# Items of 96 rows in a mixture-of-experts block, and the overflow branch behind the final norm

## The chip, the cores and the metric

The kernel runs on one core of one Trainium2 chip. The metric is device time in microseconds (us) of that core, the median of three runs.

## What is computed

One trunk layer over 512 tokens of width 1024, in float32: an input norm, a combined projection, eight heads of forgetting attention and eight of stick-breaking attention, an output projection added to the input, then a mixture of experts added to that, and a last norm. The change touches the mixture and the last norm. Cut to these:

```python
logits = t @ w_router + b_router              # 512 tokens, 32 experts
top_v, top_i = lax.top_k(logits, 4)           # each token goes to 4 experts
top_w = softmax(top_v)
# per expert e, on the rows (tokens) that chose it, however many they are:
hh  = x @ w1[e] + b1[e]                       # 1024 -> 2048
glu = minimum(hh[:, :1024], 7.0)
lin = clip(hh[:, 1024:], -7.0, 7.0)
act = glu * sigmoid(1.702 * glu) * (lin + 1.0)
y   = (act @ w2[e] + b2[e]) * weight_of_row   # 1024 -> 1024, added to its tokens
out = rmsnorm(x2 + sum of y, norm_f_g)
```

An expert gets 64 rows on average (512 x 4 / 32).

## The kernel before

**Items.** The mixture runs as a list of items, one expert's weights and up to 128 of its rows each. `run_items(MAIN)` does items 0 to 31, item e being the first 128 rows of expert e. An expert with more than 128 rows leaves the rest to items 32 and up, `run_items(REST)`, which stand in a branch that is entered only if the fullest expert has more than 128 (`fullest` writes 0 or 1 into `novi`; every engine loads that value and branches).

**One item.** GpSimd gathers the rows from `tn_scratch` with an indirect DMA (L655, indices in `gtab`; a row that doesn't exist has an index past the last token and isn't moved). TensorE turns them (`turn_x`, L2139, eight transposes of 128 columns), ScalarE copies the result to `xT_hi` rounded (L1063, L1066), VectorE writes the remainder `xT_lo` (L1596). The weights arrive in float32 in `ring` (SyncE's queue) in pieces of 128x1024; ScalarE casts each to `stage_hi` (L783), VectorE subtracts to get `stage_lo` (L1203), and `multiply` (L2189) runs six matmuls of 512 columns with it: T_hi with hi, T_lo with hi, T_hi with lo, for two banks. An item has 16 pieces of w1 and 8 of w2. Between them stand the clips (L1632, L1636), the gate (L1085), `gated` (L1644, the product), `turn_a` (L2147, eight transposes), `a_evac` (L1079) and again L1596. `y_evac` (L1093) scales by the row's weight into `yout` and GpSimd adds the rows to `x_scratch` (called `x2_d`) in memory: a copy of the indices to `sidx` (L662) and an indirect DMA (L666), then a wait for its landing.

**The order.** Each engine has its instructions in program order; the order of pieces and of the small operations between them is written by hand (`body(r)`, with `if j == ...`). The w2 pieces of item t-1 follow the w1 pieces of item t.

**The end.** The last item isn't scattered. Its result is kept on chip as `y_hi` (`last_high`, ScalarE L1168) and `y_lo` (`last_low`, VectorE L1718), and for each of four tiles of 128 tokens TensorE adds the second biases (`second_biases`, L2272) and the rows of the last item picked by a one-hot matrix (`last_expert`, L2294) in PSUM. When GpSimd has seen item 30 land and has passed the branch, it sets `all_scattered` (L772), and SyncE loads the four tiles of `x2_d` (`total(t)`, L582). VectorE adds PSUM to each (`added`, L1756), ScalarE takes the sum of squares and the root (L1185, L1187), VectorE scales (`final`, L1762, L1763), SyncE stores (L585). The branch for REST stands, on every engine, ahead of this part; on TensorE between the second biases and `last_expert`:

```python
pe.wait_ge(over_known, 1)
n_over = pe.value_load(novi[0:1, 0:1], min_val=0, max_val=1)
with pe.If(n_over > 0):
    ...                       # items 32 and up
pe.wait_ge(onehot_r, TT)
pe.wait_ge(y_ready, E)
for t in range(TT): ...       # last_expert
```

Of the kernel before, what the change touches and what calls it, by code (L numbers as in the profile page):

```python
# [20 lines left out]
F32 = mybir.dt.float32  # L21
# [30 lines left out]
OVER = S * TOPK // P - 1  # L52
# [78 lines left out]
def build(nc, x, norm1_g, w_in, b_f, g_fox, g_sb, w_out, norm2_g, w_router, b_router, w1, b1, w2, b2,  # L131
# [6 lines left out]
    with ExitStack() as ctx:  # L138
# [32 lines left out]
        gtab = sb("gtab", [P, ITEMS], I32)  # L171
        wtab = sb("wtab", [P, ITEMS])
        seltab = sb("seltab", [P, ITEMS + OVER])
        eidtab = sb("eidtab", [1, 16], I32)
        novi = sb("novi", [1, 1], I32)
        gidx = sb("gidx", [P, 1], I32)
        sidx = sb("sidx", [P, 1], I32)
        wcol = sb("wcol", [P, 1])
        last_rows = sb("last_rows", [P, 1])
# [51 lines left out]
        onehot = over("onehot", [P, S], F32R, room_at + 7168)  # L231
# [7 lines left out]
        ohslot = over("ohslot", [P, 16, P], F32R, qk_at + 16 * S)  # L239
        over_slot = in_slot("over_slot", [P, 16, P], F32R, 8)  # L240
# [14 lines left out]
        y_hi = act_hi[:, 2 * D:3 * D]  # L255
        y_lo = act_lo[:, 2 * D:3 * D]
        g2b = slot(8)[:, 0:D]
        small = slot(8)[:, D:2 * D]
        gath = qk2[:, 0, :]
        glu = qk2[:, 1, :]  # L260
        lin = qk2[:, 2, :]
        sig = qk2[:, 3, :]
        yout = qk2[:, 4, :]
# [22 lines left out]
        counts = part(2007, 32)  # L286
        most = part(2039, 1)
# [161 lines left out]
        def _(sp):  # L449
# [100 lines left out]
            sp.dma_start(gfb, norm_f_g.rearrange("(a d) -> a d", a=1).partition_broadcast(P)).then_inc(gf_in, 16)  # L550
            sp.wait_ge(over_known, 1)
# [26 lines left out]

            sp.wait_ge(split_lo, MAIN.split(E - 1, W1P + W2P - 1))
            sp.wait_ge(all_scattered, 1)  # L580
            for t in range(TT):
                sp.dma_start(total(t), x2_d[t * P:(t + 1) * P, :]).then_inc(fin_in[t], 16)  # L582
            for t in range(TT):
                sp.wait_ge(fin_ready, t + 1)
                sp.dma_start(out_d[t * P:(t + 1) * P, :], total(t)).then_inc(out_done, 16)  # L585
# [5 lines left out]
        def _(pool):  # L591
# [156 lines left out]
            def last_scatter():  # L748

                pool.wait_ge(y_ready, E)  # L750
                nc.gpsimd.tensor_copy(sidx[:], gtab[:, E - 1:E]).then_inc(sidx_copied, 1)
# [20 lines left out]
            nc.gpsimd.memset(gidx[:], 0).then_inc(all_scattered, 1)  # L772
# [3 lines left out]
        def _(act):  # L776
# [282 lines left out]
            def x_evac(t):  # L1059

                early = isinstance(t, int) and t == 0
                act.wait_ge(*((x_half, 1) if early else (x_turned, t + 1)))
                nc.scalar.copy(xT_hi[:, 0:4, :], bank[6][:].rearrange("p (k t) -> p k t", k=4)).then_inc(xT_hi_r, 1)  # L1063
                if early:
                    act.wait_ge(x_turned, 1)
                nc.scalar.copy(xT_hi[:, 4:8, :], bank[7][:].rearrange("p (k t) -> p k t", k=4)).then_inc(xT_hi_r, 1)  # L1066

            def x_next(t, h, used_at):

                if h == 0:  # L1070
                    act.wait_ge(x_turned, t + 1)
                else:
                    act.wait_ge(used, used_at)
                nc.scalar.copy(xT_hi[:, 4 * h:4 * h + 4, :], bank[6 + h][:].rearrange("p (k t) -> p k t", k=4)).then_inc(xT_hi_r, 1)

            def a_evac(t, halves=(0, 1)):
                act.wait_ge(a_turned, t + 1)
                for h in halves:
                    nc.scalar.copy(aT_hi[:, 4 * h:4 * h + 4, :], bank[6 + h][:].rearrange("p (k t) -> p k t", k=4)).then_inc(aT_hi_r, 1)  # L1079
# [7 lines left out]
            def y_evac(t, used_at):  # L1087
# [4 lines left out]
                for h in range(2):  # L1092
                    ins = nc.scalar.activation(yout[:, h * BANK:(h + 1) * BANK], bank[4 + h][:], ACT.Copy,  # L1093
# [3 lines left out]
            def run_items(run):  # L1097
# [7 lines left out]
                for j in range(W1P):  # L1105
                    if j == STAGES:
                        x_evac(q0)
                        if b == MOE0:
                            act.wait_ge(wt_mm, 1)
                            nc.scalar.copy(wtab[:, 0:E], bank[1][:, 0:E]).then_inc(wt_copied, 1)  # L1110
# [38 lines left out]
                for j in range(W2P):  # L1149
# [13 lines left out]
            def last_high(used_at):  # L1163
# [3 lines left out]
                for h in range(2):  # L1167
                    nc.scalar.activation(y_hi[:, h * BANK:(h + 1) * BANK], bank[h][:], ACT.Copy, scale=wcol[:]).then_inc(last_hi, 1)  # L1168
# [4 lines left out]
            nc.scalar.copy(b2r[0:96, :], b2raw[0:96, :]).then_inc(b2_hi, 1)  # L1173
            act.wait_ge(over_known, 1)
            n_over = act.value_load(novi[0:1, 0:1], min_val=0, max_val=1)
            last_high(MAIN.base - OPROJ_PIECES + 24 * E)
            with act.If(n_over > 0):
                act.wait_ge(over_copied, 1)
                nc.scalar.copy(wtab[:, E:ITEMS], bank[5][:, P + WIDE:P + WIDE + OVER]).then_inc(over_copied, 1)
                run_items(REST)  # L1180

            nc.scalar.preload_act_table_set("sqrt_and_others")
            for t in range(TT):
                act.wait_ge(fin_added, t + 1)
                nc.scalar.activation(squares(t), total(t), ACT.Square, accum_out=ss3[:, t:t + 1]).then_inc(fin_sq, 1)  # L1185
                act.wait_ge(fin_sq, t + 1)
                nc.scalar.activation(rs3[:, t:t + 1], ss3[:, t:t + 1], ACT.Sqrt, scale=1.0 / D, bias=epsc).then_inc(fin_rs, 1)  # L1187
# [3 lines left out]
        def _(dve):  # L1191
# [297 lines left out]
            def slots(g):  # L1489
# [10 lines left out]
                nc.vector.tensor_tensor(ohslot[:, a], iotas[:].unsqueeze(1).to_broadcast([P, TOPK * n, P]),  # L1500
# [824 lines left out]
```

## Time and profile before

| | |
|---|---|
| median of three runs | 1477.76 us (1477.41 to 1479.73) |
| the profiled execution's own time | 1478.53 us |
| its span, first to last instruction | 1476.8 us |
| TensorE busy | 1448.6 us, 98% |
| VectorE busy | 1323.5 us, 90% |
| ScalarE busy | 1114.6 us, 75% |
| mean granted TensorE clock | 0.993 |

Engines in the rows are PE (TensorE), PEld (its weight loads), DVE (VectorE), ACT (ScalarE), POOL (GpSimd) and SP (SyncE). A share of busy time is a mean over the attention, the routing, the 32 items and the end. The span runs from the first instruction to the last; 1.7 us of the execution's time lie outside it.

### The profile page before, as it was taken

What the parts mean: (1) busy time and instruction counts of PE and PEld (TensorE: products, weight loads), DVE (VectorE), ACT (ScalarE), POOL (GpSimd) and SP (SyncE); (2) the same over time, 40 slices, a digit from 0 to 9 for tenths busy, and PEclk for the clock granted to TensorE, in tenths of its full rate; (3) what the DMA queues carried; (4) which work ended last, traced back from release to release, by engine and by line L of the source; (5) the groups of instructions that cost most, each with busy time, mean ns of one, the idle gap of its engine ahead of it and who ended that gap; (6) DMA issues with size and microseconds to landing.
All of it is one profiled execution on the core that took longest, in us unless ns stands there. A gap on an engine that the chain in (4) does not pass through costs nothing.

```text
span 1476.8 us, 22343 instructions
## 1 busy us (share of the span) xinstructions
PE 1448.6 (98%) x7069; PEld 1180.6 (80%) x7069; DVE 1323.5 (90%) x1520; ACT 1114.6 (75%) x1345; POOL 325.4 (22%) x179
## 2 busy tenths in 40 slices
PE   9999999999999999999999999999999999999996
PEld 7777787787888888888888888888888888888884
DVE  5778656569999999999999999999999999999997
ACT  5668545357888888888888888888888888878885
POOL 3000000141322222222222233233222222222210
PEclk9999999989999999999999999999999999999998
DMA  8021122369999999999999999999999999999963
GB/s 258 22 65 57 30 94 67 129 225 418 417 383 384 378 378 374 375 370 376 375 369 375 374 369 380 365 371 389 367 361 373 373 378 369 369 372 379 370 220 125
DMA packets 100074, 451.32 MB, mean 306 GB/s; under 512 B 13443, under 2 KB 25731, under 8 KB 67266
## 3 DMA queue, kind: packets, MB, share of 16 engines
q1 hardware_dynamic: 90706, 434.16, 76.8%
q0 software_dynamic: 9328, 16.64, 4.5%
q8 instruction: 23, 0.38, 0.1%
q14 instruction: 17, 0.14, 0.0%
HBM read 444.66 MB, written 22.54 MB: 316 GB/s over the span
## 4 chain that ended last, share of the span: by engine, by line
PE 85%; DVE 7%; ACT 3%; DMA 2%; issue 2%; POOL 0%; SPq 0%; POOLq 0%; ACTq 0%; DVEq 0%
PE zpair L2189 46%; PE bank L2189 23%; PE bank L1889 2%; PE bank L1777 2%; PE bank L2139 2%; PE bank L2147 2%; PE bank L1779 2%; PE bank L1778 2%; DVE stage_lo L1203 1%; DVE lbuf L1283 1%; PE zpair L2158 1%; DVE pt_lo L1292 1%; DMA tn_scratch<-qk 1%; ACT stage_hi L783 1%; DMA ring<-x_scratch 0%
## 5 line engine op out<-in xcount | busy, mean ns | idle before, releaser
L1203 DVE TENSOR_TENSOR stage_lo<-ring,stage_hi 128x1024 fp32r<-128x1024 f32 x796 | 945.9, 1222 | 37.9 <-ACT stage_hi L783 8.3
L783 ACT CAST stage_hi<-ring 128x1024 fp32r<-128x1024 f32 x796 | 828.2, 1054 | 169.8 <-PE zpair L2189 139.0
L2189 PE MATMUL zpair<-stage_hi,act_hi 128*128 128x512 f32 x1024 | 322.5, 396 | 0.0
L2189 PE MATMUL zpair<-stage_lo,act_hi 128*128 128x512 f32 x1024 | 316.2, 390 | 0.4 <-DVE stage_lo L1203 0.3
L2189 PE MATMUL zpair<-stage_hi,act_lo 128*128 128x512 f32 x1024 | 316.0, 390 | 0.0
L2189 PEld LDWEIGHTS zpair<-stage_lo,act_hi 128*128 128x128 f32 x1024 | 192.1, 188 | 41.8 <-DVE stage_lo L1203 1.3
L2189 PEld LDWEIGHTS zpair<-stage_hi,act_lo 128*128 128x128 f32 x1024 | 192.2, 188 | 40.9
L2189 PEld LDWEIGHTS zpair<-stage_hi,act_hi 128*128 128x128 f32 x1024 | 187.2, 188 | 43.4 <-issue 7.9
L662 POOL COPY sidx<-gtab 128x1 int32 (+1 forms) x31 | 122.4, 3947 | 378.2 <-ACT qk L1093 378.2
L2189 PE MATMUL bank<-stage_hi,act_hi 128*128 128x512 f32 x512 | 161.2, 396 | 0.0
L2189 PE MATMUL bank<-stage_hi,act_lo 128*128 128x512 f32 x512 | 158.6, 391 | 0.0
L2189 PE MATMUL bank<-stage_lo,act_hi 128*128 128x512 f32 x512 | 157.8, 389 | 0.0
L666 POOL DMA_INDIRECT x_scratch<-qk,sidx x31 | 129.6, 4179 | 25.0 <-POOL sidx L662 25.0
L2189 PEld LDWEIGHTS bank<-stage_lo,act_hi 128*128 128x128 f32 x512 | 96.1, 188 | 21.1 <-DVE stage_lo L1203 0.4
L2189 PEld LDWEIGHTS bank<-stage_hi,act_lo 128*128 128x128 f32 x512 | 96.4, 188 | 20.5
L2189 PEld LDWEIGHTS bank<-stage_hi,act_hi 128*128 128x128 f32 x512 | 94.0, 189 | 17.6
L651 POOL COPY gidx<-gtab 128x1 int32 (+1 forms) x31 | 6.1, 198 | 402.8 <-PE bank L2139 402.8
L1596 DVE TENSOR_TENSOR act_lo<-bank,act_hi 128x512 fp32r<-128x512 f32 x128 | 82.3, 683 | 4.9 <-ACT act_hi L1063 3.5
L1777 PE MATMUL bank<-act_hi,stage_hi 128*128 128x512 f32 x184 | 76.3, 415 | 1.9 <-DVE v_lo L1247 1.9
L1779 PE MATMUL bank<-act_hi,stage_lo 128*128 128x512 f32 x184 | 72.0, 391 | 0.0
L1778 PE MATMUL bank<-act_lo,stage_hi 128*128 128x512 f32 x184 | 71.9, 391 | 0.0
L675 POOL TENSOR_TENSOR qk<-ring 128x1024 f32<-128x1024 f32 x3 | 8.1, 2725 | 273.0 <-DVE ring L1352 273.0
(297 smaller groups left out, 1450.9 us busy)
## 6 DMA issues: line engine op xcount, KB each, us to landing
ring<-in_w SPq DMA_DIRECT2D x384, 1024.0 KB, 8.0
ring<-in_w_in SPq DMA_DIRECT2D x12, 1024.0 KB, 5.3
ring<-in_w_out SPq DMA_DIRECT2D x4, 1024.0 KB, 4.9
xs_all<-in_x SPq DMA_DIRECT2D x4, 512.0 KB, 6.5
ring<-in_x SPq DMA_DIRECT2D x4, 512.0 KB, 3.7
tn_scratch<-qk SPq DMA_DIRECT2D x4, 512.0 KB, 3.5
x_scratch<-ring SPq DMA_DIRECT2D x4, 512.0 KB, 3.8
ring<-x_scratch SPq DMA_DIRECT2D x4, 512.0 KB, 6.7
```

The costliest lines, as they stand in the source:

```text
L662: nc.gpsimd.tensor_copy(sidx[:], gtab[:, i:i + 1] if isinstance(i, int) else gtab[:, bass.ds(i, 1)]).then_inc(sidx_copied, 1)
L666: nc.gpsimd.indirect_dma_start(out=x2_d[:, :], out_offset=bass.IndirectOffsetOnAxis(ap=sidx[:, 0:1], axis=0), in_=yout, in_offset=None, bo ...
L783: nc.scalar.copy(dst, src).then_inc(split_hi, 1)
L1203: nc.vector.tensor_tensor(dst, src, hi_ap.bitcast(F32), ALU.subtract).then_inc(split_lo, 1)
L1596: nc.vector.tensor_tensor(dst_lo[:, 4 * h:4 * h + n, :], bank[6 + h][:, 0:n * P].rearrange("p (k t) -> p k t", k=n), dst_hi[:, 4 * h:4 * h ...
L1777: pe.matmul(dst, w_hi, m_hi, start=start, stop=False)
L1778: pe.matmul(dst, w_hi, m_lo, start=False, stop=False)
L1779: return pe.matmul(dst, w_lo, m_hi, start=False, stop=stop)
L1889: mm = pe.matmul(obank[m][:, kb * P:S], w[:, ph % 2, kb, :], x[:, m, 4 * kb:3 * kb + TT, :].rearrange("p i q -> p (i q)"), start=kb == 0 a ...
L2139: mm = pe.transpose(bank[6 + k // 4][:, k % 4 * P:(k % 4 + 1) * P], gath[:, k * P:(k + 1) * P], identF[:])
L2147: mm = pe.transpose(bank[6 + k // 4][:, k % 4 * P:(k % 4 + 1) * P], lin[:, k * P:(k + 1) * P], identF[:])
L2189: mm = pe.matmul(bank[b0 + h][:], w[:, k, :], m[:, j % STAGES, h * BANK:(h + 1) * BANK], start=start and w is T_hi and m is stage_hi, stop ...
```

## The change

The capacity of an item, `CAP`, becomes 96 rows instead of 128, and the branch is entered if the fullest expert has more than 96. Everything that has one partition per row of an item is cut to 96 partitions, and everything that has one column per row to 96 columns, with one exception: the stationary tiles of `multiply` keep 128 columns (`w[:, k, :]`), of which the last 32 hold what was there before, and the 32 output rows that follow from them are not read. The branch moves behind the final norm and store on every engine; if it is entered, totals, sums and stores are done a second time. The order of a few steps at the end changes. The core of the diff:

```diff
+CAP = 96
+OVER = S * TOPK // CAP
...
-        gath = qk2[:, 0, :]
+        gath = qk2[0:CAP, 0, :]
...          # likewise glu, lin, sig, yout, y_hi, y_lo, gtab, wtab, onehot; ohslot has CAP columns
-                    mm = pe.transpose(bank[6 + k // 4][:, k % 4 * P:(k % 4 + 1) * P], gath[:, k * P:(k + 1) * P], identF[:])
+                    mm = pe.transpose(bank[6 + k // 4][:, k % 4 * CAP:(k % 4 + 1) * CAP], gath[:, k * P:(k + 1) * P], identF[0:CAP, 0:CAP])
...          # turn_a the same; x_evac, x_next, a_evac, turned_lo on 4 x 96 columns
-                nc.vector.tensor_scalar(novi[:], most[0:1, :], float(P), None, ALU.is_gt).then_inc(over_known, 1)
+                nc.vector.tensor_scalar(novi[:], most[0:1, :], float(CAP), None, ALU.is_gt).then_inc(over_known, 1)
...          # SyncE: totals before its branch; it waits for the landing itself
+            sp.wait_ge(split_lo, MAIN.split(E - 1, W1P + W2P - 1))
+            sp.wait_ge(scattered, 16 * (E - 1))
+            totals(0)
             sp.wait_ge(over_known, 1)
             n_over = sp.value_load(novi[0:1, 0:1], min_val=0, max_val=1)
             with sp.If(n_over > 0):
+                sp.wait_ge(out_done, 16 * TT)
...
-            sp.wait_ge(split_lo, MAIN.split(E - 1, W1P + W2P - 1))
-            sp.wait_ge(all_scattered, 1)
...          # ScalarE, the last item's w2 pieces
                     if j == 2:
-                        act.wait_ge(used, ub + 24 * n - 8)
+                        y_evac(q0 + n - 2, ub + 24 * n - 8)
                         a_evac(q0 + n - 1, (1,))
-                    if j == 3:
-                        y_evac(q0 + n - 2, ub + 24 * n - 8)
...
+            nc.scalar.preload_act_table_set("sqrt_and_others")
+            last_high(MAIN.base - OPROJ_PIECES + 24 * E)
+            roots(0)
             act.wait_ge(over_known, 1)
             n_over = act.value_load(novi[0:1, 0:1], min_val=0, max_val=1)
-            last_high(MAIN.base - OPROJ_PIECES + 24 * E)
...          # VectorE, body of the last item
+                        if j == 22 and last:
+                            gated(t)
                 body(n - 1, last=True)
-                gated(q0 + n - 1)
...
+            last_low()
+            dve.wait_ge(gf_in, 16)
+            finals(0)
             dve.wait_ge(over_known, 1)
             n_over = dve.value_load(novi[0:1, 0:1], min_val=0, max_val=1)
-            last_low()
...          # TensorE
             for t in range(3):
                 second_biases(t)
+            pe.wait_ge(onehot_r, TT)
+            pe.wait_ge(last_hi, 2)
+            for t in range(2):
+                last_expert(t, y_hi)
+            pe.wait_ge(y_ready, E)
+            for t in range(2):
+                last_expert(t, y_lo)
+            for t in range(2, TT):
+                if t == TT - 1:
+                    second_biases(t)
+                last_expert(t, y_hi)
+                last_expert(t, y_lo)
             pe.wait_ge(over_known, 1)
             n_over = pe.value_load(novi[0:1, 0:1], min_val=0, max_val=1)
             with pe.If(n_over > 0):
```

`finals(n)`, `roots(n)` and `totals(n)` hold the loops of the final norm that stood outside functions before, with their semaphores counted up by n rounds.

## Rows read from the trace of the kernel before

**Rows 1.** The page, part 1: busy us, share, instructions of each engine.

```profile
PE 1448.6 (98%) x7069; PEld 1180.6 (80%) x7069; DVE 1323.5 (90%) x1520; ACT 1114.6 (75%) x1345; POOL 325.4 (22%) x179
```

**Rows 2.** Groups of TensorE, 500 to 1300 us: busy, mean ns | idle before.

```profile
L2189 PE MATMUL zpair<-stage_hi,act_hi 128*128 128x512 f32 x730 | 229.7, 396 | 0.0
...
L2139 PE MATMUL bank<-identF,qk 128*128 128x128 f32 x184 | 23.9, 273 | 0.0
L2147 PE MATMUL bank<-identF,qk 128*128 128x128 f32 x184 | 23.8, 272 | 0.0
```

**Rows 3.** Groups of VectorE, 500 to 1300 us.

```profile
L1203 DVE TENSOR_TENSOR stage_lo<-ring,stage_hi 128x1024 fp32r<-128x1024 f32 x547 | 649.7, 1221 | 23.0
L1596 DVE TENSOR_TENSOR act_lo<-bank,act_hi 128x512 fp32r<-128x512 f32 x92 | 59.0, 683 | 0.0
```

**Rows 4.** Timeline of TensorE at two places: start us, length us, out<-moving,stationary.

```profile
288.08 0.94 PE L1949 MATMUL bank<-ones,f_sum 128*128 128x1 f32 x8
288.89 0.49 PE L1777 MATMUL zpair<-act_hi,fox_hi 128*128 128x512 f32 x1
...
824.20 1.03 PE L2147 MATMUL bank<-identF,qk 128*128 128x128 f32 x8
824.99 0.71 PE L2189 MATMUL zpair<-stage_hi,act_hi 128*128 128x512 f32 x2
```

**Rows 5.** Timeline of GpSimd over one item.

```profile
801.62 1.06 POOL L655 DMA_INDIRECT qk<-tn_scratch,gidx  x1 [0.78 <-POOL gidx L651]
813.83 4.02 POOL L662 COPY sidx<-gtab 128x1 int32 x1 [11.16 <-ACT qk L1093]
818.66 4.23 POOL L666 DMA_INDIRECT x_scratch<-qk,sidx  x1 [0.81 <-POOL sidx L662]
836.77 1.06 POOL L655 DMA_INDIRECT qk<-tn_scratch,gidx  x1 [0.78 <-POOL gidx L651]
```

**Rows 6.** The page: GpSimd's DMA queue, and the stores (us to landing).

```profile
q0 software_dynamic: 9328, 16.64, 4.5%
...
out<-ring SPq DMA_DIRECT2D x4, 512.0 KB, 2.7
```

**Rows 7.** DMA of 555.5 to 567.5 us, the gather of item 8: packets, MB.

```profile
q0 software_dynamic: 144, 0.36, 7.6%
```

**Rows 8.** Timeline of VectorE at the end.

```profile
1435.54 5.76 DVE L1203 TENSOR_TENSOR stage_lo<-ring,stage_hi 128x1024 fp32r<-128x1024 f32 x5
1441.21 1.22 DVE L1644 SCALAR_TENSOR_TENSOR qk<-qk 128x1024 f32<-128x1024 f32 x1
...
1465.60 1.29 DVE L1756 TENSOR_TENSOR ring<-bank,ring 128x512 f32<-128x512 f32 x2 [0.57 <-DMA ring<-x_scratch]
...
1472.37 1.28 DVE L1763 SCALAR_TENSOR_TENSOR ring<-ring,cols,qk 128x1024 f32<-128x1024 f32 x1
```

**Rows 9.** Timelines of TensorE, ScalarE and GpSimd at the end, one after another.

```profile
1442.49 1.09 PE L2147 MATMUL bank<-identF,qk 128*128 128x128 f32 x8 [0.79 <-DVE qk L1644]
...
1459.73 1.11 PE L2294 MATMUL bank<-act_hi,onehot 128*128 128x512 f32 x2 [2.20 <-issue]
...
1445.05 0.59 ACT L1079 CAST act_hi<-bank 128x512 fp32r<-128x512 f32 x1
...
1446.48 1.28 ACT L1093 ACTIVATE qk<-bank,wcol 128x512 f32<-128x512 f32 x2
...
1447.82 1.16 POOL L662 COPY sidx<-gtab 128x1 int32<-128x1 int32 x1 [28.77 <-ACT qk L1093]
1449.74 1.77 POOL L666 DMA_INDIRECT x_scratch<-qk,sidx  x1 [0.76 <-POOL sidx L662]
```

**Rows 10.** The chain that ended last, at the end: start us, length us.

```profile
1449.74 6.03 DMA x_scratch<-qk,sidx
...
1457.09 0.35 SPq L582
...
1458.47 7.10 DMA ring<-x_scratch
```

More of the change, by code:

```diff
@@ L238, in build @@
         tT = [slot(6 + h).rearrange("p (k t) -> p k t", k=4) for h in range(2)]
-        ohslot = over("ohslot", [P, 16, P], F32R, qk_at + 16 * S)
-        over_slot = in_slot("over_slot", [P, 16, P], F32R, 8)
+        ohslot = over("ohslot", [P, 16, CAP], F32R, qk_at + 16 * S)
+        over_slot = in_slot("over_slot", [P, 16, CAP], F32R, 8)
         pay_at = qk_at + 48 * S + 4 * 1208
@@ L285, in build @@
         w_lo = part(916, 16)
-        counts = part(2007, 32)
-        most = part(2039, 1)
+        counts = part(2013, 32)
+        most = part(2045, 1)
         pick = part(952, 256).rearrange("p (a e) -> p a e", e=E)
@@ L576, in _ @@
                                  w2_d[bass.ds(el, 1), k:k + 2].rearrange("e k p n -> p (e k) n")).then_inc(full[z], 16)
-            sp.wait_ge(split_lo, MAIN.split(E - 1, W1P + W2P - 1))
-            sp.wait_ge(all_scattered, 1)
[L581 to L585, printed above, removed]
+                sp.wait_ge(all_scattered, 1)
+                totals(1)
+                sp.wait_ge(out_done, 32 * TT)
             sp.wait_ge(out_done, 16 * TT)
@@ L750, in last_scatter @@
                 pool.wait_ge(y_ready, E)
+                for t in range(TT):
+                    pool.wait_ge(fin_in[t], 16)
                 nc.gpsimd.tensor_copy(sidx[:], gtab[:, E - 1:E]).then_inc(sidx_copied, 1)
@@ L1747, in _ @@
                 run_items(REST)
[L1749 to L1770 removed]
+                finals(1)
         @block.tensor
@@ L2076, in row_table @@
                 for a in range(a0, TOPK * (GROUPS[g][-1] + 1)):
-                    mm = pe.matmul(bank[0][:, 0:E], ohslot[:, a, :], pays[g][:, a - a0, 0, :],
+                    mm = pe.matmul(bank[0][0:CAP, 0:E], ohslot[:, a, :], pays[g][:, a - a0, 0, :],
                                    start=a == 0, stop=a == 4 * TOPK - 1)
@@ L2267, in _, with second_biases, last_expert @@
             run_items(MAIN)
-            def second_biases(t, start=True):
+            def second_biases(t, stop=False):
                 for h in range(2):
-                    pe.matmul(bank[FIN[t] + h], wdT[0:96, t * P:(t + 1) * P], b2r[0:96, h * BANK:(h + 1) * BANK], start=start, stop=not start)
+                    mm = pe.matmul(bank[FIN[t] + h], wdT[0:96, t * P:(t + 1) * P], b2r[0:96, h * BANK:(h + 1) * BANK], start=True, stop=stop)
+                return mm
+            def last_expert(t, m):
+                for h in range(2):
+                    mm = pe.matmul(bank[FIN[t] + h], onehot[:, t * P:(t + 1) * P], m[:, h * BANK:(h + 1) * BANK],
+                                   start=False, stop=m is y_lo)
+                if m is y_lo:
+                    mm.then_inc(fin_mm, 1)
             pe.wait_ge(b2_lo, 1)
@@ L2279, in _ @@
             with pe.If(n_over > 0):
-                for t in range(3):
-                    second_biases(t, False)
-                pe.wait_ge(y_ready, E)
-                pe.wait_ge(onehot_r, 2 * TT)
+                pe.wait_ge(fin_added, TT)
                 over_table()
@@ L2286, in _ @@
                 pe.wait_ge(y_ready, ITEMS)
-                for t in range(3):
-                    second_biases(t)
-            def last_expert(t):
-                for m in (y_hi, y_lo):
-                    for h in range(2):
-                        mm = pe.matmul(bank[FIN[t] + h], onehot[:, t * P:(t + 1) * P], m[:, h * BANK:(h + 1) * BANK],
-                                       start=False, stop=m is y_lo)
-                mm.then_inc(fin_mm, 1)
-            pe.wait_ge(onehot_r, TT)
-            pe.wait_ge(y_ready, E)
-            for t in range(TT):
-                if t == 3:
-                    second_biases(t)
-                last_expert(t)
+                for t in range(TT):
+                    second_biases(t, True).then_inc(fin_mm, 1)
 _INS = ["x", "norm1_g", "w_in", "b_f", "g_fox", "g_sb", "w_out", "norm2_g", "w_router", "b_router",
```

172 lines of the change are left out of this document (88 added, 84 removed).

## The prediction

> **What bounds the kernel now.** I read the page's first part, then TensorE's and VectorE's groups over the stretch in which only items run, then the end in timelines and in the chain. The page shows TensorE busy for 98% of the span [rows 1]. That alone is weak, so the groups: over 800 us of items the matmuls and transposes of TensorE have 0.0 us of idle time ahead of them [rows 2], while VectorE has 23 us before its pieces [rows 3]. So an item costs what TensorE issues for it, and the period of one is 35.15 us, from gather to gather [rows 5]. Work taken from VectorE, ScalarE or GpSimd inside an item is worth nothing there. At the end it is otherwise: after TensorE's last piece the chain goes through GpSimd's transfer of item 30 (6.03 us), the issue of the loads at 1457.09, a load that lands at 1458.47 + 7.10 = 1465.57, and VectorE's sums and scalings, back to back from 1465.60 to 1473.65 [rows 8, 10]. The start of these loads sets the end of the kernel.
>
> **Is the branch taken?** That comes first, since it is worth most. Running the reference's own router on the inputs gives 34 to 88 rows per expert, the fullest being expert 8. The trace agrees: the transfer of item 8 moves 0.36 MB, which is 88 rows of 4 KB [rows 7], and all of GpSimd's queue 16.64 MB [rows 6], close to 2048 rows gathered and 1998 added (16.57 MB). 88 is under 96, so 32 items run after as before. That the sums on the chip differ in the last bits can move a token or two, not eight.
>
> **The items.** `multiply` keeps 128 stationary columns and 512 moving ones: 768 pieces cost the same. VectorE's remainders fall from 512 to 384 columns; from 683 ns at 512 and 1221 ns at 1024 columns [rows 3] a column costs 1.05 ns, so each of the four per item saves 0.13 us, and ScalarE's copies likewise about 0.1 us. TensorE waits for none of them [rows 2], so 0. The transposes have 96 moving columns for 128 and 96 rows, with 128 stationary columns as before, 512 of them in all (16 per item). Does one get shorter? Eight with 128 moving columns take 824.20 to 824.99, 99 ns each; eight matmuls with one moving column but as wide a stationary tile take 288.08 to 288.89, 101 ns each [rows 4]. So what is moved doesn't count here, and the weight load does; it keeps its width. I take 0. The other bound is a saving by columns, a quarter of 99 ns if all of it were column time: 25 ns x 512 = 12.7 us; more plausible is column time at the 2.4 GHz clock, 32 columns or 13.3 ns, 6.8 us. The first is ruled out by the one-column rows; the second stays as a rival.
> The Trainium skill ("TensorE: Matmul & The Clock Gate", LDWEIGHTS) says that a load takes time by its columns, 128 / 1.2 = 107 ns, whatever its rows; the two rows agree within 8 ns, and by it the sum has 0 here. The same page (Back-to-back issue gap) gives N / 2.4 + 2.5 ns for a matmul alone, by which the transposes would give 6.8 us back.
>
> **The start of the mixture.** `ohslot` is a quarter narrower and the first gather lists 96 indices. The gather waits for the tokens to land in memory, not for VectorE, and its issue costs about 1.06 us [rows 5]; a quarter of that is 0.27 us at most. I take 0.2, with bounds 0 and 0.6 for the few narrower table matmuls.
>
> **The end, step by step.** (1) `gated` moves ahead of the last of five pieces on VectorE. Those five take 5.76 us, 1.135 us apart, and the product starts at 1441.21 [rows 8]; it will start near 1440.08 and end near 1441.30. TensorE waited 0.79 us for it before the transposes at 1442.49 [rows 9], so they start 0.8 us earlier. The piece that now comes after it is done near 1442.5; TensorE needs it some 0.9 us into piece 23, near 1443.3: no new wait. (2) On ScalarE `y_evac` of item 30 goes before the second `a_evac` and one piece: 1446.48 - 1445.05 = 1.43 us [rows 9]. With (1) and 0.1 us of a narrower copy it ends at 1446.48 + 1.28 - 2.4 = 1445.4 for 1447.76. What is queued behind it, `a_evac` and piece 3, is done near 1445.8 and 1446.8, and TensorE reaches the pieces that need them near 1449.6 and 1448.2. (3) GpSimd copies its indices and issues the transfer: 1.16 + 0.76 + 1.77 us, landing 1449.74 + 6.03 - 1451.51 = 4.26 us after the issue's end [rows 9, 10]. With these the landing is at 1453.4 for 1455.77. (4) The way from there to the loads, 1457.09 - 1455.77 = 1.3 us [rows 10], is GpSimd's load of the flag, its branch and a memset; it is gone, SyncE waits for the landing itself. So the loads would start 3.6 us earlier. But step (3) is not safe: inside the items the same copy takes 4.02 and the same issue 4.23 us [rows 5], and only at the end 1.16 and 1.77. In the new order the copy falls on one piece of VectorE and then a `turned_lo`, the issue on two pieces back to back. I take 0.5 us off: 3.1 us.
> The Trainium skill ("SBUF — State Buffer", SBUF: two separate sides) says that GpSimd and a VectorE operation with two SBUF inputs lock each other out for a whole instruction. The two lengths of one copy of 128 values agree with it; by it the copy is let in at `turned_lo`, whose input is PSUM, near 1446.3.
>
> (5) Do the sums follow the loads? TensorE waits for no branch now (2.20 us of idle time before 1459.73 [rows 9]); its last product of tile 2 is ready near 1459.5, under 1462 even at half the speed, where the load of tile 2 lands at 1465.57 - 3.1 = 1462.5. VectorE needs 10.4 us for four sums and four scalings, from about 1459.0, so no earlier than 1469.4, under 1473.65 - 3.1 = 1470.55. The table load, 1.3 us on ScalarE, lies between its last piece and the last matmul, in an idle stretch of over 3 us. (6) The branches now run while the last store is under way: 2.7 us to landing [rows 6] cover a branch of 2.20 us at most [rows 9]. 0; without the cover up to 2.2 us would be added.
>
> Sum against the profiled execution: 1478.53 - 3.1 - 0.2 = 1475.2. The median of the runs lies 0.77 us lower, so the forecast is 1474.5 us.
>
> **The rivals.** The measurement tells 0.2% of 1477.76, 3.0 us, from no change: faster is below 1474.8, slower above 1480.7.
> - *GpSimd is locked out at the end as in the items.* With 4.02 and 0.8 us but 1.77 for the issue the loads start at 1445.4 + 4.02 + 0.8 + 1.77 + 4.26 = 1456.3, 0.8 us earlier: 1476.8. With 4.23 too, 1458.7, 1.6 us later than before: 1479.2. For it: 29 copies of 31 take this long. Against: the one at this place didn't.
> - *The transposes get shorter by their columns.* 1474.5 - 6.8 = 1467.7. Against: the one-column rows.
> - *Slower: more than 96 rows for an expert on the chip.* Then 21 more items at 35.15 us run, with a second end of about 20 us (1457 to 1476.8) and a first load that nothing hides: 1474.5 + 738 + 20 + some 15, about 2250 us. It decides from the 97th row of one expert. Against: 88.
> - *The branches outlast the store.* 1474.5 + 1 to 2.2: 1475.5 to 1476.7.
> - *Nothing moves*, since the end is bound by something I don't see: 1477.8.
>
> **How the numbers follow.** Forecast 0.50, own range 1473.0 to 1475.8, of which four fifths lie under 1474.8, since the margins of the issue are on the early side as well (3.6 instead of 3.1). GpSimd locked out 0.22; transposes 0.10; branches 0.08; nothing 0.07; more items 0.03. Faster: 0.40 + 0.10 + 0.02 from a mild case of the branches, 0.52. Slower: 0.03 for the items and 0.02 for a lockout together with uncovered branches, 0.05. Same: the rest, 0.43. The range leaves out the extra items and the low end of the transposes: 1469.5 to 1477.6.
>
> **What would show it.** Right: L2139 and L2147 eight at 0.79 us and a period of 35.15; `y_evac` of item 30 ending at 1445.4 less the 0.2 of the start; the loads issued near 1454; no idle time of TensorE between L2272 and L2294 of over 0.3 us; VectorE's last scaling at 1470.3. Wrong: gathers less than 35.0 us apart; a copy of indices of 4 us at 1445; a last store that landed before the span's end by over 0.5 us; more than 31 gathers behind the first.

## The result, and the profile after

The changed kernel takes 1466.81 us, median of four runs (1466.33 to 1467.1), against 1477.59 us for the old one on the same chip: ratio 0.9925, 95% interval 0.9908 to 0.9942. It is 10.8 us faster; the forecast was 3.3 us and its range ended at 1469.5. The profiled execution took 1467.1 us with a span of 1465.2 us.

The page after, parts 1 and 3. They answer to [rows 1, 6].

```profile
PE 1432.4 (98%) x7069; PEld 1165.2 (80%) x7069; DVE 1306.8 (89%) x1520; ACT 1100.8 (75%) x1345; POOL 381.0 (26%) x178
...
q0 software_dynamic: 7312, 16.63, 5.0%
```

TensorE issues as many instructions as before and is busy for 16 us less. GpSimd is busy for 56 us more although it copies fewer indices: by its timelines 28 of the 31 copies to `sidx` take 7.58 us for 4.02 (108 us more over all 31), the issues behind them mostly 1.7 us for 4.2 (71 less), and the gathers' issues 1.78 for 1.06. TensorE waits for none of it there (0.0 us of idle time in the groups below). GpSimd's queue moves the same 16.6 MB in 2016 packets fewer: 63 indirect transfers with 32 rows fewer each make 2016. Rows that don't exist, and move nothing, still cost packets.

The groups over 500 to 1300 us, of TensorE and of VectorE; they answer to [rows 2, 3].

```profile
L2206 PE MATMUL zpair<-stage_hi,act_hi 128*128 128x512 f32 x737 | 232.1, 396 | 0.0
...
L2156 PE MATMUL bank<-identF,qk 96*128 96x96 f32 x184 | 19.0, 246 | 0.0
```

```profile
L1610 DVE TENSOR_TENSOR act_lo<-bank,act_hi 128x384 fp32r<-128x384 f32 x92 | 46.6, 547 | 0.0
```

The wide products are unchanged at 396 ns. The length of a transpose in the trace went from 273 to 246 ns. Their spacing is read better from where the next group starts (TensorE's timeline, one item):

```profile
818.65 0.82 PE L2164 MATMUL bank<-identF,qk 96*128 96x96 f32 x8
819.26 0.70 PE L2206 MATMUL zpair<-stage_hi,act_hi 128*128 128x512 f32 x2
```

Eight take 0.61 us where eight took 0.79 [rows 4]: 76 ns each for 99. GpSimd's timeline over one item, and its last gather; they answer to [rows 5]:

```profile
830.89 1.78 POOL L663 DMA_INDIRECT qk<-tn_scratch,gidx  x1 [0.80 <-POOL gidx L659]
843.07 7.58 POOL L670 COPY sidx<-gtab 96x1 int32 x1 [10.39 <-ACT qk L1103]
851.46 1.71 POOL L674 DMA_INDIRECT x_scratch<-qk,sidx  x1 [0.81 <-POOL sidx L670]
...
865.65 1.78 POOL L663 DMA_INDIRECT qk<-tn_scratch,gidx  x1 [0.79 <-POOL gidx L659]
...
1352.42 1.78 POOL L663 DMA_INDIRECT qk<-tn_scratch,gidx  x1 [0.79 <-POOL gidx L659]
```

From the fourth gather (379.35; before 380.10) to the last (1352.42; before 1363.91) there are 28 periods: 34.75 us each for 35.14. The items gave 10.7 us there, 0.38 us each, of which two times eight transposes are 2 x 0.18 = 0.36.

The end, VectorE and then GpSimd; they answer to [rows 8, 9]:

```profile
1436.91 0.14 DVE L1626 COPY wcol<-wtab 96x1 f32<-96x1 f32 x1
1436.98 3.48 DVE L1217 TENSOR_TENSOR stage_lo<-ring,stage_hi 128x1024 fp32r<-128x1024 f32 x3
1440.38 0.14 DVE L1738 CAST last_rows<-gtab 96x1 f32<-96x1 int32 x1
1440.55 1.22 DVE L1740 TENSOR_TENSOR act_hi<-b2raw,act_hi 32x1024 fp32r<-32x1024 f32 x1
...
1433.13 1.18 POOL L670 COPY sidx<-gtab 96x1 int32<-96x1 int32 x1 [24.95 <-ACT qk L1103]
1435.08 6.69 POOL L674 DMA_INDIRECT x_scratch<-qk,sidx  x1 [0.78 <-POOL sidx L670]
```

And the chain that ended last, which answers to [rows 10]:

```profile
1435.08 10.77 DMA x_scratch<-qk,sidx
...
1445.91 0.34 SPq L555
...
1446.29 5.65 DMA ring<-x_scratch
...
1459.98 1.28 DVE ring L1764
```

The transfer lands at 1435.08 + 10.77 = 1445.85 and the loads are issued at 1445.91; before, 1.3 us lay between. The branch is gone from the path. But the issue takes 6.69 us where it took 1.77, and that ate what the end had won. From the last gather to the end of the span it was 112.89 us before and is 112.78 us now.

So two things are to be explained: why the transposes got shorter against [rows 4], and why the issue got longer.

### The profile page after: what moved, and what is told of

It reads as the page before. It is cut to its first block, busy times and chain, and to the rows that moved or that the text cites. A ratio compares the mean times of both kernels' runs of the same rounds, so it can differ in the third digit from the quotient of the medians.

```text
span 1465.2 us, 22341 instructions
## 1 busy us (share of the span) xinstructions
PE 1432.4 (98%) x7069; PEld 1165.2 (80%) x7069; DVE 1306.8 (89%) x1520; ACT 1100.8 (75%) x1345; POOL 381.0 (26%) x178
## 4 chain that ended last, share of the span: by engine, by line
PE 86%; DVE 7%; ACT 3%; DMA 2%; issue 1%; POOL 0%; SPq 0%; ACTq 0%; POOLq 0%; DVEq 0%
PE zpair L2206 47%; PE bank L2206 24%; PE bank L1906 2%; PE bank L1794 2%; PE bank L1796 2%; PE bank L1795 2%; PE bank L2156 2%; PE bank L2164 1%; DVE stage_lo L1217 1%; DVE lbuf L1297 1%; PE zpair L2175 1%; DMA x_scratch<-qk,sidx 1%; DVE pt_lo L1306 1%; DMA tn_scratch<-qk 1%; DVE lbuf L1293 0%
## 5 line engine op out<-in xcount | busy, mean ns | idle before, releaser
L670 POOL COPY sidx<-gtab 96x1 int32 (+1 forms) x31 | 230.3, 7428 | 350.4 <-ACT qk L1103 350.4
L659 POOL COPY gidx<-gtab 96x1 int32 (+1 forms) x31 | 6.5, 211 | 364.1 <-PE bank L2156 364.1
L1610 DVE TENSOR_TENSOR act_lo<-bank,act_hi 128x384 fp32r<-128x384 f32 x128 | 65.1, 547 | 4.8 <-ACT act_hi L1073 4.4
L674 POOL DMA_INDIRECT x_scratch<-qk,sidx x31 | 58.2, 1876 | 25.4 <-POOL sidx L670 25.4
```

Source lines behind the costliest of these rows:

```text
L670: nc.gpsimd.tensor_copy(sidx[:], gtab[:, i:i + 1] if isinstance(i, int) else gtab[:, bass.ds(i, 1)]).then_inc(sidx_copied, 1)
L674: nc.gpsimd.indirect_dma_start(out=x2_d[:, :], out_offset=bass.IndirectOffsetOnAxis(ap=sidx[:, 0:1], axis=0), in_=yout, in_offset=None, bo ...
L1610: nc.vector.tensor_tensor(dst_lo[:, 4 * h:4 * h + n, 0:CAP], bank[6 + h][:, 0:n * CAP].rearrange("p (k t) -> p k t", k=n), dst_hi[:, 4 * h ...
```

## The experiments

Experiments 2 and 10 are small programs without the layer. Each of the others starts from the changed kernel; its ratio is to the old kernel's time on the same chip, and the lengths of single steps are from one profiled execution of each.

**1. Transposes of 128 again.**

```diff
-mm = pe.transpose(bank[6 + k // 4][:, k % 4 * CAP:(k % 4 + 1) * CAP], gath[:, k * P:(k + 1) * P], identF[0:CAP, 0:CAP])
+mm = pe.transpose(bank[6 + k // 4][:, k % 4 * P:(k % 4 + 1) * P], qk2[:, 0, k * P:(k + 1) * P], identF[0:P, 0:P])
```

The same for `lin`; the copies out of the banks still take 96 columns of each 128.

> The changed kernel, with turn_x and turn_a alone put back to 128 rows and 128 identity columns (rows 96 to 127 of the source hold leftovers that are not used afterwards); the copies behind them still take 96 columns of each block. Theory A: the transposes themselves got shorter, 0.61 for 0.79 us a group of eight. Then a group is back at 0.79 us, the period of an item at 35.15 us, and the time rises by 512 x 22.5 ns = 11.5 us to about 1478. Rival B: the shorter work of VectorE and ScalarE is what shortens an item, and the transposes only look shorter: the period stays at 34.77 us and the time at 1467.

Measured: 1474.86 us (1472.51 to 1476.48, 10 runs), ratio 0.9981, interval 0.9971 to 0.999, which doesn't touch that of the changed kernel. The period is back at 35.14 us ((1363.55 - 379.75) / 28). With the transposes alone undone, the whole gain of the items is gone. The end, which is the new one, is short here: from the last gather to the span's end 109.55 us, 3.3 less than before. In this execution the issue took 3.23 us.

**2. What a transpose costs, by itself.** A program without the layer: streams of 32 transposes, each behind eight wide products.

```python
def turned(rows, cols):
    for i in range(32):
        pe.transpose(bank[...][0:cols, ...rows columns], data[0:rows, ...cols columns], ident[0:rows, 0:rows])
```

> A kernel of its own (its output is zeros, nothing of the reference is computed): streams of 32 equal instructions on TensorE between fillers of eight 512-column matmuls. Float32 transposes of 128, 96, 64 and 32 rows with 128 stationary columns, then with 96 and 64 stationary columns; plain float32 matmuls with 1 to 128 moving columns, and rounded float32 ones with 32 to 512. Theory A1 (each of load and stream counts in a float32 transpose): 128 rows 99 ns, 96 rows 76, 64 rows about 53, 32 rows about 30 to 53. Rival A2 (the rows of the stationary tile set the load): then a plain float32 matmul with 1 moving column falls from 101 to 76 ns with 96 rows as well. Rival A3 (a floor by the width of the stationary tile): no fall below some 76 ns, and a fall with 96 stationary columns.

TensorE's timeline; a stream ends where the next group starts:

```profile
25.80 3.65 PE L58 MATMUL bank<-ident,data 128*128 128x128 f32 x32
29.21 2.09 PE L54 MATMUL bank<-rm,rw 128*128 128x512 f32 x8
31.14 2.80 PE L58 MATMUL bank<-ident,data 96*128 96x96 f32 x32
33.73 2.09 PE L54 MATMUL bank<-rm,rw 128*128 128x512 f32 x8
35.75 2.23 PE L58 MATMUL bank<-ident,data 64*128 64x64 f32 x32
37.91 2.12 PE L54 MATMUL bank<-rm,rw 128*128 128x512 f32 x8
39.96 2.17 PE L58 MATMUL bank<-ident,data 32*128 32x32 f32 x32
42.06 2.12 PE L54 MATMUL bank<-rm,rw 128*128 128x512 f32 x8
44.01 3.65 PE L58 MATMUL bank<-ident,data 128*96 128x128 f32 x32
47.42 2.09 PE L54 MATMUL bank<-rm,rw 128*128 128x512 f32 x8
```

The granted clock was 1.00 over these streams. Rows turned 128, 96, 64, 32: 107, 81, 67 and 66 ns each. With 128 rows it is 107 ns again with 96 stationary columns, and with 64 (49.35 to 52.76), and 96 rows with 96 stationary columns take 81 ns (54.69 to 57.28). So what is turned counts, 0.8 ns a row from 128 to 96, down to a floor of 66 ns, and the width of the stationary tile doesn't. In a transpose the number of rows and the number of moving columns (those of the identity) are one and the same, so no run tells which of the two it is. The streams of plain products behind these ran at a clock that had partly fallen to its lower level (mean 0.62 from 60 to 100 us), so they were measured again (experiment 10).

**3. Stationary tiles of 96 columns** in `multiply` and the first biases, which the change leaves at 128:

```diff
-mm = pe.matmul(bank[b0 + h][:], w[:, k, :], ...
+mm = pe.matmul(bank[b0 + h][0:CAP, :], w[:, k, 0:CAP], ...
```

> The changed kernel with stationary tiles of 96 columns in multiply and in the bias matmuls, outputs on 96 partitions. Theory C (the weight load hides under 512 moving columns): spacing of L2206 stays at 226.7 ns, time 1467 within 2 us. Rival D (the 13 ns over 512 / 2.4 = 213 ns are a part of the load): spacing falls to some 223 ns, 15 us less. Rival E: a narrower tile loads in a slower way, so that the spacing rises; then the time is above 1470.

Measured: 1475.02 us (1474.15 to 1477.3, 10 runs), ratio 0.9987, interval 0.9977 to 0.9997: 8 us slower than with the unread columns. TensorE's groups, 500 to 1300 us:

```profile
L2206 PE MATMUL zpair<-stage_hi,act_hi 128*96 128x512 f32 x728 | 229.7, 396 | 0.0
L2206 PE MATMUL zpair<-stage_hi,act_lo 128*96 128x512 f32 x728 | 226.5, 392 | 0.0
```

The period is 35.02 us ((1359.08 - 378.48) / 28), 0.27 more than in the changed kernel: 7.5 us over 28 items. A narrower stationary tile made the wide products slower, by about 2 ns each (144 in an item).

**4. The new end with the old items:**

```diff
-CAP = 96
-OVER = S * TOPK // CAP
+CAP = 128
+OVER = S * TOPK // CAP - 1
```

> The changed kernel with CAP 128: the new order of the end with items as before. It splits the change in two. If the items gave nearly all (31 periods of 0.38 us = 11.8 us), this is 1477 to 1479 and not distinguishable from the kernel before. If the end gave its forecast 3.1 us, it is 1474.5. By the trace of the changed kernel the transfer of item 30 was issued 12.7 us earlier within the kernel but took 10.8 us to land for 6.0, which would leave the end some 0.5 us: 1477.2.

Measured: 1475.59 us (1473.05 to 1477.25, 10 runs), ratio 0.9989, interval 0.9979 to 0.9999. In its profiled execution the issue took 3.51 us and the tail from the last gather was 109.92 us, 3.0 less than before. By its ratio the kernel gains less, 1.6 us, and the runs lie 4.2 us apart.

**5. `y_evac` of item 30 back behind the second `a_evac` and one piece** on ScalarE, as in the old order:

```diff
 if j == 2:
-    y_evac(q0 + n - 2, ub + 24 * n - 8)
+    act.wait_ge(used, ub + 24 * n - 8)
     a_evac(q0 + n - 1, (1,))
+if j == 3:
+    y_evac(q0 + n - 2, ub + 24 * n - 8)
```

> The changed kernel with y_evac of item 30 back behind piece 3 and the second a_evac, as before the change. Theory F: what delays the landing is that GpSimd's issue meets a run of VectorE operations with both inputs in SBUF and ends only with the run (1441.77, when L1740 ends). Then an issue 1.4 us later ends at the same place and lands at the same time: 1466.8, no change. Rival G: the issue's length is its own; then the landing and the end move 1.4 us later: 1468.2.

Measured: 1467.99 us (1466.8 to 1470.41, 4 runs), ratio 0.993, interval 0.9912 to 0.9947, no different from the change. GpSimd:

```profile
1434.28 6.05 POOL L670 COPY sidx<-gtab 96x1 int32<-96x1 int32 x1 [26.28 <-ACT qk L1103]
1441.11 1.81 POOL L674 DMA_INDIRECT x_scratch<-qk,sidx  x1 [0.78 <-POOL sidx L670]
```

Now the copy is the long one, up to 1440.33, and the issue is short. The loads start at 1446.95 instead of 1445.91. The copy starts 1.15 us later than in the changed kernel and the loads 1.04 us later. Theory F had the issue end at the same place as before; it ended 1.15 us later, because the copy was kept out in its place, which neither side had expected. So in this execution the order on ScalarE is worth about 1 us (the medians are 1.2 us apart, but the intervals overlap), and how long the pair of copy and issue takes depends on when GpSimd is let in.

**6. The indices of item 30 copied ahead of the wait for its result:**

```diff
-pool.wait_ge(y_ready, i + 1)
+early = isinstance(i, int) and i == E - 2
+if not early:
+    pool.wait_ge(y_ready, i + 1)
 nc.gpsimd.tensor_copy(sidx[:], gtab[:, i:i + 1] ...).then_inc(sidx_copied, 1)
 pool.wait_ge(sidx_copied, i + 1)
+if early:
+    pool.wait_ge(y_ready, i + 1)
```

> The changed kernel with the copy of the indices of item 30 (L670) done before GpSimd waits for y_evac, so that the issue starts at once, near 1433.2 for 1435.1, while VectorE is still short of turned_lo at 1434.2. Theory F: the issue gets in at turned_lo and lands near 1439.5 instead of 1445.8; then TensorE and VectorE bound the end (sums from 1446.3, 10.4 us more): 4 us less, 1463. Rival G: 1.9 us less, 1465. If the issue misses the gap: 1466.8.

Measured: **1462.11 us** (1460.69 to 1462.98, 4 runs), ratio 0.9895, interval 0.9878 to 0.9912. GpSimd and VectorE:

```profile
1432.11 1.69 POOL L678 DMA_INDIRECT x_scratch<-qk,sidx  x1 [18.09 <-ACT qk L1107]
```

```profile
1432.41 0.55 DVE L1614 TENSOR_TENSOR act_lo<-bank,act_hi 128x384 fp32r<-128x384 f32 x1
...
1444.65 1.29 DVE L1761 TENSOR_TENSOR ring<-bank,ring 128x512 f32<-128x512 f32 x2 [1.03 <-PE bank L2299]
```

The issue starts 3 us earlier, lies over a subtraction whose one input is PSUM, and takes 1.69 us. The loads start at 1438.31. VectorE's first sum now waits for TensorE: that is what bounds the end here.

**7. VectorE's pieces held until the issue is out**, by a wait behind piece 4:

```diff
 # GpSimd, behind the issue of item 30's transfer
+if isinstance(i, int) and i == E - 2:
+    pool.sem_inc(gath_zero, 1)
 # VectorE, the last eight pieces, behind piece 4
+if j == 4 and b == MOE0:
+    dve.wait_ge(gath_zero, 2)
```

> The changed kernel with one more wait: VectorE holds piece 4 of the last item until GpSimd has issued the transfer of item 30. The issue starts at 1435.1 as before. Theory F: VectorE stands still for 0.4 us or so, the issue takes 1.0 to 1.8 us for 6.7, the landing is near 1441 for 1445.8, and the time falls by 4 us to 1463. Rival G: the issue takes 6.7 us on its own, VectorE and with it TensorE stand still for over 5 us: 1471 or more.

Measured: 1466.48 us (1465.12 to 1467.7), ratio 0.9925, interval 0.9908 to 0.9942. The issue took 6.70 us again, from 1433.60 to 1440.30, and VectorE had no idle time, though piece 4 came near 1434.3: the wait was met ahead of the issue's end, by the increment queued behind the issue on GpSimd, so it held nothing. The run tests nothing of what it was made for; it serves as the changed kernel on the chip of experiments 5 to 8, 4.4 us above experiment 6.

**8. Experiments 6 and 7 together:**

> The copy of indices early and VectorE holding piece 3 until the issue is out. Theory F: issue at 1433.2, out by 1435, landing near 1439.3, earlier than anything needs it: 1462.5 to 1463.5, no better than the better of the two alone, since TensorE's last products (from 1446.2) and VectorE's 10.4 us bound the end then. Rival G: above 1470.

Measured: 1461.85 us (1461.01 to 1462.53), ratio 0.9892, interval 0.9875 to 0.9909; the issue took 1.68 us. The wait adds nothing to the early copy.

**9. The run of pieces broken earlier.** Two kernels, in which the copy of the last expert's indices and the four row marks stand behind piece 4 or behind piece 5 of the last eight, not behind piece 7:

```diff
 if j == 4:
     weights(q0 + n - 1)
+if j == 4 and b == MOE0:        # the second kernel: j == 5
+    row_marks()                 # last_rows copied and marked here
```

> The changed kernel, with VectorE's copy of the last expert's indices and its four row marks (operations with one input in SBUF, about 0.2 us each) moved from behind the last piece to behind piece 4 of the last eight, so that the run of pieces with two SBUF inputs is broken there. In the changed kernel GpSimd's issue of item 30's transfer starts at 1435.08 and takes 6.69 us, to the end of that run. Theory (the issue is let in only where the run ends or breaks): it starts as before and ends at the marks, near 1437 to 1438.2, so it takes 2 to 3.2 us; the landing and the loads come some 3.5 us earlier, and the time falls by 3 us, near 1464 us (the end may be bound by TensorE from there, as in the run with the early index, which gave 1462.1). Rival (the issue takes 6.7 us for another reason, its place in the queue or the 96 rows): 6.5 to 6.9 us again and 1466.8 us. Rival (a break of a few small operations isn't enough, as the copy of one column wasn't): it ends at the end of the later run, near 1441 to 1442, and the time is 1466.8 us as well; the next run tells these two apart.

> As the run before, with the marks one piece (1.13 us) later, behind piece 5. Theory: the issue ends 1.1 us later than in the run before, near 1438.2 to 1439.3, after 3.1 to 4.3 us, and the time is about 1 us longer than there, 1465 us, unless the other waits of the end hide it. Rival (another reason): 6.7 us and 1466.8 us. If both runs show the issue ending where the two-input run starts again after the marks, the marks are what lets it in.

Measured: 1462.98 us (1461.55 to 1464.51), ratio 0.9909, interval 0.9892 to 0.9925; and 1464.05 us (1463.6 to 1464.29), ratio 0.9913, interval 0.9897 to 0.993. The first kernel, VectorE and GpSimd:

```profile
1436.68 0.14 DVE L1626 COPY wcol<-wtab 96x1 f32<-96x1 f32 x1
1436.74 0.14 DVE L1732 CAST last_rows<-gtab 96x1 f32<-96x1 int32 x1
1436.91 0.87 DVE L1735 TENSOR_SCALAR onehot<-iotas,last_rows 96x128 fp32r<-96x128 f32 x4
...
1434.84 3.23 POOL L674 DMA_INDIRECT x_scratch<-qk,sidx  x1 [0.78 <-POOL sidx L670]
```

The second:

```profile
1436.80 1.21 DVE L1217 TENSOR_TENSOR stage_lo<-ring,stage_hi 128x1024 fp32r<-128x1024 f32 x1
1437.93 0.14 DVE L1732 CAST last_rows<-gtab 96x1 f32<-96x1 int32 x1
1438.11 0.87 DVE L1735 TENSOR_SCALAR onehot<-iotas,last_rows 96x128 fp32r<-96x128 f32 x4
...
1434.89 4.43 POOL L674 DMA_INDIRECT x_scratch<-qk,sidx  x1 [0.77 <-POOL sidx L670]
```

The issue starts at the same place in both and as in the changed kernel, and ends at 1438.07, 1439.32 and 1441.77. In the second kernel it follows the moved operations, as expected. In the first the copy to `wcol` stands right ahead of them, so it may as well be that copy that let the issue in. That the issue takes 6.7 us for a reason of its own is ruled out. The interval of each kernel's ratio overlaps with the changed kernel's; the traces, not the times, decide this.

**10. Products beside transposes at full clock.** Streams of eight behind 32 wide products:

> No layer: streams of eight TensorE instructions each behind 32 wide ones that keep the clock up, so that plain float32 products can be read beside float32 transposes at one clock; the rest of the reference is left out. It asks why the eight one-column products of the old kernel, 101 ns each, were a wrong guide for the transposes. Theory (a product of plain float32 goes through TensorE as two passes, each record being a pass with a floor; a transpose is one pass of about 0.83 ns a moved row with a floor near 66 ns): transposes again 107, 81 and 66 ns with 128, 96 and 32 rows; a one-column float32 product shows two records of some 65 to 105 ns whatever the rows and the stationary width, and a 128-column product 100 to 115 ns for each record. Rival (one floor by the stationary tile's width for products, so that 96 stationary columns are cheaper than 128): the one-column product with 96 stationary columns is a quarter shorter. The last four streams hold 64 wide rounded products with 128, 96, 128 and 96 stationary columns and 512 moving ones: theory, from the kernel with 96 stationary columns, which was 0.27 us per item slower over 768 products: the 96-column ones are no faster and at most 1 ns slower. Rival (a smaller tile is never slower): equal within 0.1 ns.

The granted clock was 1.00 throughout. TensorE's timeline (a plain float32 product leaves two records, so 16 for 8):

```profile
37.56 0.82 PE L58 MATMUL bank<-ident,data 96*128 96x96 f32 x8
38.17 7.53 PE L54 MATMUL bank<-rm,rw 128*128 128x512 f32 x32
45.63 0.68 PE L58 MATMUL bank<-ident,data 32*128 32x32 f32 x8
46.24 7.55 PE L54 MATMUL bank<-rm,rw 128*128 128x512 f32 x32
...
53.63 1.84 PE L63 MATMUL bank<-data 128*128 128x1 f32 x16
55.33 7.56 PE L54 MATMUL bank<-rm,rw 128*128 128x512 f32 x32
...
80.90 1.95 PE L63 MATMUL bank<-data 128*128 128x128 f32 x16
82.60 7.51 PE L54 MATMUL bank<-rm,rw 128*128 128x512 f32 x32
...
108.11 1.44 PE L63 MATMUL bank<-data 128*96 128x1 f32 x16
109.42 7.54 PE L54 MATMUL bank<-rm,rw 128*128 128x512 f32 x32
```

A record of a product with 128 stationary columns takes 1.70 / 16 = 106 ns, with 1 moving column or with 128. With 96 stationary columns it takes 1.31 / 16 = 82 ns. With 96 rows and 128 stationary columns it stays at 107 ns (89.95 to 91.66), so the rows of the stationary tile don't count in a product. My expectation had one floor for products whatever their tile; the rival was right: a narrow product costs by its stationary width, a transpose by what is turned.

The transposes in streams of eight didn't come out as expected (107, 81 and 66 ns). They took 99 ns with 128 rows (29.42 to 30.21) and 76 with 96, the same as in the two kernels, but 76 with 32 rows too. So the floor of 66 ns is that of a long stream; in a group of eight between wide products, as the kernel has them, 32 rows were no cheaper than 96. What sets that, no run shows.

The last four streams, 64 wide rounded products each, took 14.51, 14.72, 14.52 and 14.72 us with 128, 96, 128 and 96 stationary columns: 226.7 and 230.0 ns. That is 3.3 ns more for the narrower tile, over the 1 ns that I had allowed, and it confirms the direction of experiment 3. Why, no run shows.

## Why the prediction was wrong

**The step that failed** is in the part on the items: "what is moved doesn't count here, and the weight load does; it keeps its width. I take 0", with the bound of 12.7 us "ruled out by the one-column rows". The transposes are worth 22.5 ns x 512 = 11.5 us by the timelines. Between the fourth and the last gather the items gave 10.7 us, and experiment 1 takes all of that away. The one-column rows of [rows 4] are of another kind of instruction: a record takes 101 ns because its stationary tile has 128 columns, and since a plain float32 product leaves two records, the eight are four products, which the prediction took for eight. The transposes take 99 ns because 128 rows are turned. Two different limits give nearly the same length at 128, and I read one from the other. The upper bound, a quarter of 99 ns, was nearly exact; the rival of 13.3 ns a transpose, 6.8 us, was too small. The prediction's own sign of being wrong, gathers less than 35.0 us apart, came true at 34.75.

The Trainium skill ("TensorE: Matmul & The Clock Gate", LDWEIGHTS) has the load go by the stationary columns, P / 1.2 in ns: 107 and 80 ns for 128 and 96. The narrow products agree with 106 and 82 ns. The transposes don't: with 128 stationary columns they take 81 and 66 ns in experiment 2. Here the measurement decides; the rule is not one for float32 transposes.

**The second miss** is step (3), and a rival named it. The prediction kept 1.77 us for the issue of item 30's transfer; it took 6.69. The end won 3.0 to 3.3 us where the issue took 3.2 to 3.5 us (experiments 1 and 4), close to the forecast 3.1, and 0.1 us in the changed kernel. The rival gave 1476.8 or 1479.2 us for a copy, or a copy and an issue, as long as in the items; it came to 9.05 us from the start of the copy to the end of the issue, and that took 8.64 us (1433.13 to 1441.77). But it had the copy as the first victim; the copy took 1.18 us and the issue was the victim, so the price was right in part by luck. The two misses have opposite signs: 1474.5 - 11.5 + 3.0 is 1466.0 us, for 1466.8 measured.

When is the issue let in? GpSimd's spans are rough in a profile, but the ends can be checked by the landings: with 96 rows the transfer lands 3.9 to 4.1 us behind the issue's end whether the issue took 1.8 or 6.7 us, with 128 rows 4.3 us. In VectorE's timeline I looked for the operation that the issue's end follows, among those whose inputs aren't both wide tiles in SBUF. Starts in us, from the timelines of one execution each:

| kernel | issue starts | `wcol` copied | `last_rows` copied | issue ends | behind which start |
|---|---|---|---|---|---|
| before | 1449.74 | 1449.98 | 1453.45 | 1451.51 | `wcol`, 1.53 |
| experiment 4 | 1445.22 | 1447.20 | 1450.67 | 1448.73 | `wcol`, 1.53 |
| experiment 1 | 1446.75 | 1448.59 | 1452.05 | 1449.98 | `wcol`, 1.39 |
| 9, piece 4 | 1434.84 | 1436.68 | 1436.74 | 1438.07 | `wcol`, 1.39 (`last_rows`, 1.33) |
| after | 1435.08 | 1436.91 | 1440.38 | 1441.77 | `last_rows`, 1.39 |
| experiment 3 | 1442.27 | 1444.11 | 1447.58 | 1448.97 | `last_rows`, 1.39 |
| experiment 7 | 1433.60 | 1435.44 | 1438.91 | 1440.30 | `last_rows`, 1.39 |
| 9, piece 5 | 1434.89 | 1436.73 | 1437.93 | 1439.32 | `last_rows`, 1.39 |

In the table the end lies 1.39 us behind the start of a small copy with 96 rows and 1.53 us with 128; in experiments 6 and 8 it lies 1.39 us behind the PSUM subtraction (1432.41 to 1433.80, 1432.95 to 1434.34). In experiment 5 it is the copy that is kept out; it ends 0.12 us behind the start of the `last_rows` copy (1440.21), and the issue 1.29 us behind that of the row marks. All this fits an issue that needs about 1.4 us from the moment it is let in, and that is let in at a break in the run of subtractions with two SBUF inputs. The Trainium skill ("SBUF — State Buffer", SBUF: two separate sides) says that the pair of ports is held for a whole instruction and "the other fully blocks"; the table agrees, but it shows a block over several instructions back to back (after: 1435.08 to 1440.38, five pieces and one copy), not over one.

What stays open: in four rows of the table the issue's end fits the `wcol` copy, in four that copy was passed over, with the issue started 1.83 or 1.84 us ahead of it in both sorts (experiment 1, after). VectorE's next operation starts only 0.06 or 0.07 us behind `wcol`, and 0.17 or 0.18 us behind `last_rows`, which let GpSimd in every time that it was still kept out; whether the shorter break is what makes `wcol` fail, no run tests. Inside the items the same thing repeats. Before, the copy to `sidx` ends 0.12 us behind the start of `wcol` (813.83 + 4.02 = 817.85, for 817.73). In the changed kernel it starts at 843.07 and passes over two small operations of VectorE:

```profile
846.92 0.14 DVE L1626 COPY wcol<-wtab 96x1 f32 x1
846.99 2.35 DVE L1217 TENSOR_TENSOR stage_lo<-ring,stage_hi 128x1024 fp32r<-128x1024 f32 x2
849.25 0.22 DVE L1621 CAST sel<-seltab 128x128 fp32r x1
```

It ends at 850.65, where two pieces start 1.21 us apart (849.39 and 850.60) that are 1.13 us apart back to back, and it took 7.58 us in 28 items alike. So where the timing repeats, the outcome does; what in the timing decides it is open. One execution of each kernel says nothing of how often it happens at the end. The times of experiments 1 and 4 spread over 4 us, which a changing outcome would explain, but that is only argued.

**Point by point, the rest.**
- The branch isn't taken: right, no gather past the last.
- VectorE's remainders: 683 to 547 ns, 0.14 us each for 0.13, and worth nothing: right.
- The wide products unchanged, 396 ns: right.
- The start: the first gather lies 0.27 us earlier (320.17 for 320.44), forecast 0.2. That isn't shown: in the eight other kernels with 96 rows it lies anywhere from 319.01 to 320.63.
- Steps (1) and (2): from the start of the transposes of item 31's activations to the end of `y_evac` it was 1442.49 to 1447.76, 5.27 us, and is 1429.53 to 1433.06, 3.53 us, with no idle time ahead; forecast 3.7: right. "No new wait" was a little off: TensorE waits 0.28 us for VectorE ahead of 1432.04.
- Step (4), 1.3 us of branch and memset: gone, right.
- Step (5): the sums follow the loads, right up to where the issue gets short; in experiment 6 they are bound by TensorE.
- Step (6), branches behind the last store at 0: a little off. From the start of VectorE's last scaling to the end of the span it was 4.43 us before [rows 8] and is 5.22 us after, and 5.1 to 5.4 in the experiments: 0.7 to 1.0 us more, every time. The last store is issued 1.31 us behind that start in both (1473.68, 1461.29); it lands after 2.7 us before and after 3.5 us now, 3.4 to 3.7 in the experiments, so the loss is in the store's landing. In that window the queue of kind `instruction` (q14) moves 4 packets in every kernel with the new end and none before. That the branches slow the store by this is likely, but no run takes it apart.

## What to carry to other kernels

An instruction that a trace lacks is not to be priced by one of another kind that happens to take as long at one size: measure it, or keep the full bound in the range. A chain through a GpSimd transfer that falls on VectorE's long runs of operations with two SBUF inputs has no fixed length: take what GpSimd can do early out of it (the index copy ahead of the wait: 1462.1 us for 1466.5 to 1466.8 here), or leave a break in VectorE's run where the issue falls. And a stationary tile may be left at 128 columns with a part unread: narrower was slower, in the kernel and by itself.

## What the runs showed of the hardware

- A float32 transpose in a stream of 32 takes 107, 81, 67, 66 ns for 128, 96, 64, 32 rows; the stationary width doesn't count (experiment 2). In a group of eight between wide products it takes 99, 76, 76 ns for 128, 96, 32 rows (experiment 10).
- A plain float32 product leaves two records; with few moving columns each takes 106 ns with 128 stationary columns, with 128 rows or 96, and 82 ns with 96 stationary columns (experiment 10).
- A wide rounded product (512 moving columns) takes 226.7 ns with 128 stationary columns and 230.0 with 96 (experiment 10).
- At the end of the kernel the issue of an indirect transfer of 96 rows ends 1.39 us (once 1.29) after a break in VectorE's run, after 1.7 to 6.7 us in all. A semaphore increment queued behind it on GpSimd came before that end (experiment 7).
- Rows whose index is out of range move no bytes but make packets: 144 a transfer with 128 indices [rows 7], 112 with 96 (the transfer of item 30 in the changed kernel).
